# Gathering the two vectors of each retrieved expert by separate transfers into separate rings

## The chip, the cores and the metric

The kernel runs on one core of a Trainium2 chip. The metric is the device time of one execution in microseconds (us); less is better. The core's engines are TensorE (PE; its weight loads are listed as PEld), VectorE (DVE), ScalarE (ACT), GpSimd (POOL) and SyncE (SP), and 16 DMA engines move data between the chip's main memory and the on-chip memory.

## The reference, cut to what matters

One layer on 1024 tokens of width 1024: a token mixer (projection, convolution branch, stick-breaking attention, gates, output projection, layer norm) gives `x1`, and then a retrieval of single-neuron experts works on it. The change touches only the retrieval:

```
for each block of 128 tokens:                      # 8 blocks
    for each head:                                 # 8 heads
        idx, gate = top 16 of 128*128 product keys # per token
        u  = expert_u[idx]                         # 16 rows of 1024 float32 per token
        vv = expert_v[idx]                         # 16 rows of 1024 float32 per token
        act = gelu(dot(x1, u))
        y += sum over the 16 of gate * act * vv
    x = layer_norm(alpha * x1 + y)
```

Each token has its own experts, so nothing is reused between tokens.

## The kernel before

**Stages.** The first 890 us compute `x1`: projections, convolution, attention, gates. From there to the end runs the retrieval: 8 token blocks x 8 heads = 64 heads (`t` counts them), each with 16 slots (`s`), so 1024 slots in all. The 128 tokens of a block lie on the 128 partitions.

**One slot.** `expert_u` and `expert_v` are concatenated on the host to rows of 2048 floats (`uv_d`). GpSimd issues one indirect transfer for each slot (L477): 128 rows of 8 KB, one for each partition, 1 MB, into slot `s % 8` of `ring`, 8 x 8 KB a partition (`RING` = 8). VectorE multiplies the u half by `x1` and sums it (L1190, `dots`, which writes the product over the u half), two slots for each signal `dots_done`. ScalarE applies gelu and the gate (L911, L913) and writes a diagonal matrix of the weights (L920). TensorE multiplies this diagonal with the v half (L672, `experts`, two matmuls of 512 columns for each slot) and adds to `y` in PSUM, then signals `expert_used[s % 8]`. GpSimd waits for that signal before it fills the ring's slot again, so that a slot is held until both its dot product and its matmuls are done. Each gather goes through `wait_alone`, a wait on a register's value.

**Indices.** GpSimd turns the 16 indices of a head into integers in two casts of 8 (L472) and waits for each. The indices of head `t + 1` are found during head `t`: TensorE makes queries and scores between its expert matmuls (`queries` L648, `query_transposes` L656, `scores` L664), and VectorE finds the top 16 between its dot products: `topk_half` after slots 5 and 7, `topk_pairs` after slot 9, `expert_index` after slot 11, whose last instruction (L1177) releases GpSimd.

**Block ends.** After the 16 slots of a block's last head VectorE waits for TensorE's last matmuls and does the second layer norm (`finish`, L1201, L1114 to L1121). In block 0 the heads also carry the output projection (`wout_mm`, L631) and first layer norm (`x1_block`) of the next blocks, and SP loads 1 MB of query weights and 0.5 MB of `x` for each head.

Of the kernel before, what the change touches and what calls it, by code (L numbers as in the profile page):

```python
# [30 lines left out]
D = 1024  # L31
# [3 lines left out]
HALF = 512  # L35
# [9 lines left out]
TOPK = 16  # L45
# [3 lines left out]
RING = 8  # L49
DIAGS = 4  # L50
START = 1
KB = 256


C_A, C_G, C_Q, C_K = 0, CC, 2 * CC, 3 * CC
# [47 lines left out]
    return (0, 1, 2, 3, 6, 7)[u % Z_BANKS]  # L103


def build(nc, xT_d, x_d, w_proj_d, w_v_d, w_mix_d, w_out_d, w_q_d, keys_d, uv_d, cols_d, bv_d,
          b_out_d, ln1_g_d, ln1_b_d, ln2_g_d, ln2_b_d, out_d):
    ctx = ExitStack()
    with ctx:
# [22 lines left out]
        def at(kib, *shape):  # L132
            n = math.prod(shape)
            arena, first = (arena_low, 0) if kib < LOW else (arena_high, LOW)
            flat = arena[:, int((kib - first) * KB):int((kib - first) * KB) + n]
            if len(shape) == 1:
                return flat
            if len(shape) == 2:
                return flat.rearrange("p (a b) -> p a b", b=shape[1])
            return flat.rearrange("p (a b c) -> p a b c", b=shape[1], c=shape[2])  # L140
# [63 lines left out]
        q_nat = at(63, 2 * P)  # L204
        gates = at(57, NB, PH * TOPK)
        w_q = at(64, PH, KD, 2 * P)
        ring = at(128, RING, 2 * D)
        idx_f = at(192, TOPK)
        top_v = at(192.25, 2, TOPK)
        soft = at(193, TOPK)  # L210
# [110 lines left out]
        shifted = sem("shifted")  # L321
        exp_ready = sem("exp_ready")
        gates_ready = sem("gates_ready")
        gathered = [sem(f"gathered{r}") for r in range(RING)]
        dots_done = sem("dots_done")
        gelu_step = sem("gelu_step")
        diag_ready = sem("diag_ready")
# [78 lines left out]
        @block.gpsimd  # L406
        def _(pool):
            for s in (psum_read + expert_used + mixed +
                      [pre_read, wout_done, conv_done, att_done, sp_done, suffix_done, av_done, acc_done, out_read, z_done, x1_ready, q_ready,
                       qT_ready, score_ready, y_read, idx_ready, idx_copied, x1T_psum]):  # L410
                pool.sem_inc(s, START)
            pool.sem_inc(stored, 16 * START)
            pool.memset(conv_in[:, 0:PAD], 0.0).then_inc(pad_ready, 1)
            pool.memset(mean_w, 1.0 / CONV).then_inc(consts, 1)
            pool.memset(one_row[0:1, :], 1.0).then_inc(consts, 1)
            pool.memset(neg_ones, -1.0).then_inc(consts, 1)
            pool.memset(zeros[:, :], 0.0).then_inc(consts, 1)
            pool.memset(tri, -1.0).then_inc(pool_step, 1)
            pool.iota(iota_i[:, :], pattern=[[1, TOPK]], base=0, channel_multiplier=0).then_inc(consts, 1)
            pool.wait_ge(pool_step, 1)  # L420
            pool.affine_select(out=tri, in_=tri, compare_op=ALU.is_ge, fill=0.0, base=0,
                               pattern=[[-1, P]], channel_multiplier=1).then_inc(consts, 1)


            for j in range(4):
                pool.wait_ge(w1_rounded, j + 1)
                nc.gpsimd.tensor_tensor(w1_lo_r[:, j, :, :], w_ring[:, j, :, :], w1_hi_r[:, j, :, :].bitcast(F32),
                                        ALU.subtract).then_inc(w1_split, 1)
            with pool.Fori(1, CC) as it:
                for j in range(4):  # L430
                    wait_alone(pool, w1_rounded, it * 4 + j + 1, consts)
                    nc.gpsimd.tensor_tensor(w1_lo_r[:, j, :, :], w_ring[:, j, :, :], w1_hi_r[:, j, :, :].bitcast(F32),
                                            ALU.subtract).then_inc(w1_split, 1)
            for k in range(KD):
                pool.wait_ge(wv_rounded, k + 1)
                nc.gpsimd.tensor_tensor(wv_lo_r[:, k, :], w_v[:, k, :], wv_hi_r[:, k, :].bitcast(F32),
                                        ALU.subtract).then_inc(wv_split, 1)

            pool.wait_ge(var_done, 1)
            pool.wait_ge(psum_read[3], START + 6)
            pool.memset(q_pair[DH:P, 0, :], 0.0).then_inc(q_zeroed, 1)
            pool.memset(q_pair[0:DH, 1, :], 0.0).then_inc(q_zeroed, 1)
            with pool.Fori(0, PAIRS) as p:
                order = sorted([(u, 0) for u in DIAG_NO] + [(u + 1.5, 1) for u in DIAG_NO])
                for key, what in order:
                    u = int(key) if what == 0 else int(key - 1.5)
                    Q, kb, hd = UNITS[u]
                    c0 = kb * P - Q * HALF  # L450
                    if what == 0:
                        wait_alone(pool, sp_done, START + p * NU + u + 1, consts)
                        tile, signal = sp[:, u % 3, c0:c0 + P], sp_masked
                    else:
                        wait_alone(pool, att_done, START + p * NU + u + 1, consts)
                        tile, signal = att[:, u % 3, c0:c0 + P], att_masked
                    pool.affine_select(out=tile, in_=tile, compare_op=ALU.is_gt, fill=0.0, base=0,  # L457
                                       pattern=[[1, P]], channel_multiplier=-1).then_inc(signal, 1)


            pool.memset(ident, 0.0).then_inc(pool_step, 1)
            pool.wait_ge(pool_step, 2)
            pool.affine_select(out=ident, in_=ident, compare_op=ALU.not_equal, fill=1.0, base=0,
                               pattern=[[-1, P]], channel_multiplier=1).then_inc(consts, 1)


            with pool.Fori(0, NB * PH) as t:
                wait_alone(pool, idx_ready, START + t + 1, consts)
                for s in range(TOPK):
                    if s % RING == 0:  # L470

                        pool.tensor_copy(idx_now[:, s:s + RING],  # L472
                                         idx_f[:, s:s + RING]).then_inc(idx_copied, 1)
                        wait_alone(pool, idx_copied, START + t * 2 + (s // RING + 1), consts)

                    wait_alone(pool, expert_used[s % RING], START + t * 2 + s // RING, consts)
                    pool.indirect_dma_start(  # L477
                        out=ring[:, s % RING, :], out_offset=None, in_=uv_d,
                        in_offset=bass.IndirectOffsetOnAxis(ap=idx_now[:, s:s + 1], axis=0),
                    ).then_inc(gathered[s % RING], 16)  # L480


        @block.tensor
        def _(pe):
# [182 lines left out]

            def experts(t, g):
                for s in range(2 * g, 2 * g + 2):
                    pe.wait_ge(diag_ready, t * TOPK + s + 1)  # L670
                    for h in range(2):
                        last = nc.tensor.matmul(ps[:, 4 + h, :], diag[:, s % DIAGS, :],  # L672
                                                ring[:, s % RING, D + h * HALF:D + (h + 1) * HALF],
                                                start=False, stop=False, skip_group_check=True)
                    last.then_inc(expert_used[s % RING], 1)

# [57 lines left out]
        def _(act):  # L734
# [171 lines left out]

            def expert_weights(t, g, steps):

                act.wait_ge(dots_done, t * (TOPK // 2) + g + 1)
                s0 = 2 * g  # L910
                steps.link(nc.scalar.activation(gcol[:, s0:s0 + 2], hcol[:, s0:s0 + 2], ACT.Gelu))  # L911
                for s in (s0, s0 + 1):
                    last = nc.scalar.activation(wcol[:, s:s + 1], gcol[:, s:s + 1], ACT.Copy,  # L913
                                                scale=gates_flat[:, bass.ds(t * TOPK + s, 1)])
                steps.link(last)
                for s in (s0, s0 + 1):

                    f = s - DIAGS
                    act.wait_ge(expert_used[f % RING], START + t * 2 + (f // RING + 1 if f >= 0 else 0))
                    nc.scalar.activation(diag[:, s % DIAGS, :], ident, ACT.Copy,  # L920
                                         scale=wcol[:, s:s + 1]).then_inc(diag_ready, 1)
# [62 lines left out]
        def _(dve):  # L984
# [201 lines left out]

            def dots(b, t, g):
                for s in range(2 * g, 2 * g + 2):
                    dve.wait_ge(gathered[s % RING], (t * 2 + (s // RING + 1)) * 16)
                    last = nc.vector.scalar_tensor_tensor(  # L1190
                        out=ring[:, s % RING, 0:D], in0=x1[:, b, :], scalar=1.0, in1=ring[:, s % RING, 0:D],
                        op0=ALU.mult, op1=ALU.mult, accum_out=hcol[:, s:s + 1])
                last.then_inc(dots_done, 1)

# [112 lines left out]
```

## Time and profile before

| | |
|---|---|
| median of 3 runs | 3706.95 us (3705.57 to 3712.73) |
| profiled execution, span first to last instruction | 3699.8 us |
| median less span: what lies around it | 7.15 us |
| busy in the span | PE 84%, DVE 61%, ACT 37%, POOL 36% |
| DMA | 1133.49 MB, mean 306 GB/s over the span |

The profile gives the profiled execution by its span alone. Its page lists busy time, groups of instructions by source line with the idle time before them and what ended it, and the DMA queues. Busy time doesn't count the issuing and waiting of an engine, and a DMA_INDIRECT of POOL is the time in which GpSimd prepares a gather, not the transfer itself. The trace also answers with waits, timelines and busy time by window.

### The profile page before, as it was taken

How to read it: one execution, taken by the hardware profiler on the slowest of the kernel's cores; microseconds unless marked ns; L12 is line 12 of the kernel's file. 1: busy time of each engine (PE TensorE's matmuls, PEld its weight loads, DVE VectorE, ACT ScalarE, POOL GpSimd, SP SyncE). 2: the span in 40 equal slices, each digit the busy share in tenths (PEclk: the TensorE clock that was granted, in tenths of full speed). 3: DMA queues.
4: the chain of work that ended last, by engine and by line, in shares of the span. 5: the costliest groups of instructions: out<-in, count | busy, mean ns of one | idle time of the engine just before them, and what ended most of it. 6: DMA issues, size and time to landing. Idle time of an engine off the chain costs nothing. (4 is left out here: it accounts for less than half of the span.)

```text
span 3699.8 us, 39202 instructions
## 1 busy us (share of the span) xinstructions
PE 3119.5 (84%) x8608; PEld 1576.3 (43%) x8608; DVE 2257.1 (61%) x4803; ACT 1372.5 (37%) x3639; POOL 1341.2 (36%) x1320
## 2 busy tenths in 40 slices
PE   9989999996999888878887888788788878877886
PEld 7754436663444333333333333334333334333332
DVE  6973331113777666666666676666667666666765
ACT  3117761111444333333433333343333433333342
POOL 2301110001444344434444444444344534444443
PEclk9999999997999999999999999999999999999999
DMA  3000001106999999999999999999999989998998
GB/s 143 28 17 1 0 13 38 51 17 251 376 382 383 392 374 410 401 375 392 400 408 362 400 412 396 368 401 408 381 389 408 403 362 405 409 407 354 406 395 338
DMA packets 158001, 1133.49 MB, mean 306 GB/s; under 512 B 17554, under 2 KB 17682, under 8 KB 23443
## 3 DMA queue, kind: packets, MB, share of 16 engines
q0 software_dynamic: 147456, 1073.81, 71.4%
q1 hardware_dynamic: 10514, 59.34, 4.2%
q8 instruction: 12, 0.20, 0.0%
q14 instruction: 19, 0.15, 0.0%
HBM read 1128.88 MB, written 4.19 MB: 306 GB/s over the span
## 5 line engine op out<-in xcount | busy, mean ns | idle before, releaser
L672 PE MATMUL ps<-arena_high 128*128 128x512 f32 x4096 | 1942.0, 620 | 486.0 <-ACT arena_high L920 485.7
L477 POOL DMA_INDIRECT arena_high<-uv_dram,idx_now x1024 | 1138.6, 1112 | 1165.6 <-PE ps L672 926.8
L1190 DVE SCALAR_TENSOR_TENSOR arena_high<-arena_low,arena_high 128x1024 f32<-128x1024 f32 x1024 | 1225.1, 1223 | 546.3 <-DMA arena_high<-uv_dram,idx_now 525.9
L672 PEld LDWEIGHTS ps<-arena_high 128*128 128x128 f32 x4096 | 769.6, 196 | 1544.5 <-issue 795.2
L911 ACT ACTIVATE gcol<-hcol 128x2 f32<-128x2 f32 x512 | 103.6, 202 | 1167.3 <-DVE arena_high L1190 1166.6
L472 POOL CAST idx_now<-arena_high 128x8 uint32<-128x8 f32 x128 | 96.3, 753 | 748.0 <-DVE arena_high L1177 747.8
L920 ACT ACTIVATE arena_high<-arena_high,wcol 128x128 f32<-128x128 f32 x1024 | 355.2, 394 | 32.8
L913 ACT ACTIVATE wcol<-gcol,arena_low 128x1 f32<-128x1 f32 x1024 | 245.5, 286 | 71.2 <-ACT gcol L911 9.4
L648 PE MATMUL ps<-arena_low 128*128 (+1 forms) x1024 | 240.0, 389 | 12.7 <-ACT arena_low L886 10.0
L648 PEld LDWEIGHTS ps<-arena_low 128*128 128x128 f32 x1024 | 198.5, 195 | 65.3 <-issue 37.1
L174 PE MATMUL ps<-x_hi_bytes,w_bytes 128*128 128x512 f32 x512 | 200.3, 391 | 0.0
L1007 DVE SCALAR_TENSOR_TENSOR arena_low<-arena_low,cols 128x1024 f32 x120 | 177.8, 1482 | 17.5 <-DVE arena_low L1003 0.6
L911 ACT ACT_TABLE_LOAD x120 | 154.0, 1283 | 4.3 <-issue 1.7
L1145 DVE MAX8 arena_high<-arena_low 128x8 f32<-128x128 f32 x128 | 37.5, 293 | 180.5 <-ACT arena_low L899 180.5
L1036 DVE SCALAR_TENSOR_TENSOR arena_low<-ps,arena_low 128x512 f32<-128x512 f32 (+3 forms) x96 | 53.6, 558 | 144.8 <-ACT arena_low L814 144.8
L1089 DVE SCALAR_TENSOR_TENSOR arena_low<-ps,cols,arena_low 128x512 f32<-128x512 f32 x16 | 12.0, 751 | 197.7 <-PE ps L619 197.7
L631 PE MATMUL ps<-arena_low 128*128 128x512 f32 x256 | 116.5, 600 | 7.7 <-DMA arena_low<-w_out_dram 7.7
L899 ACT ACTIVATE arena_low<-ps 128x256 f32<-128x256 f32 x64 | 24.5, 383 | 249.7 <-PE ps L664 249.7
L457 POOL TENSOR_SCALAR_AFFINE_SELECT arena_low<-arena_low 128x128 f32<-128x128 f32 x128 | 40.9, 330 | 199.9 <-ACT arena_low L822 101.7
L619 PE MATMUL ps<-arena_low,arena_high 128*128 128x512 f32 x256 | 112.4, 592 | 0.0
L172 PE MATMUL ps<-x_hi_bytes,w_hi_bytes 128*128 128x512 f32 x256 | 101.2, 395 | 12.1 <-DVE x_lo_bytes L989 8.8
L172 PE MATMUL ps<-x_hi_bytes,w_bytes 128*128 128x512 f32 x256 | 105.8, 413 | 3.0 <-DVE w_bytes L1081 3.0
(144 smaller groups left out, 2776.1 us busy)
## 6 DMA issues: line engine op xcount, KB each, us to landing
arena_high<-uv_dram,idx_now POOLq DMA_INDIRECT x1024, 11.0
arena_low<-w_q_dram SPq DMA_DIRECT2D x15, 1024.0 KB, 11.2
arena_high<-w_mix_dram SPq DMA_DIRECT2D x8, 1536.0 KB, 6.4
arena_high<-w_proj_dram SPq DMA_DIRECT2D x16, 512.0 KB, 3.3
arena_high<-xT_dram SPq DMA_DIRECT2D x8, 512.0 KB, 7.8
arena_low<-w_out_dram SPq DMA_DIRECT2D x2, 2048.0 KB, 9.5
arena_low<-x_dram SPq DMA_DIRECT2D x8, 512.0 KB, 7.7
out_dram<-arena_low SPq DMA_DIRECT2D x8, 512.0 KB, 7.8
```

The costliest lines, as they stand in the source:

```text
L172: nc.tensor.matmul(out, w_hi, x_hi, start=first, stop=False)
L174: return nc.tensor.matmul(out, w_lo, x_hi, start=False, stop=last)
L477: pool.indirect_dma_start(out=ring[:, s % RING, :], out_offset=None, in_=uv_d, in_offset=bass.IndirectOffsetOnAxis(ap=idx_now[:, s:s + 1], ...
L619: last = nc.tensor.matmul(ps[:, 4 * h + 2 + y, :], w_mix[:, 1 - j, o:o + P], src[:, k, cs], start=(k == 0), stop=(k == CC - 1))
L631: last = nc.tensor.matmul(ps[:, 6 + h, :], mix_blk[:, k, :], w_out[:, k, h * HALF:(h + 1) * HALF], start=(k == 0), stop=(k == KD - 1))
L648: last = nc.tensor.matmul(ps[:, 2, 0:2 * P], x1T[:, k, :], w_q[:, place, k, :], start=(k == 0), stop=(k == KD - 1))
L672: last = nc.tensor.matmul(ps[:, 4 + h, :], diag[:, s % DIAGS, :], ring[:, s % RING, D + h * HALF:D + (h + 1) * HALF], start=False, stop=Fa ...
L911: steps.link(nc.scalar.activation(gcol[:, s0:s0 + 2], hcol[:, s0:s0 + 2], ACT.Gelu))
L913: last = nc.scalar.activation(wcol[:, s:s + 1], gcol[:, s:s + 1], ACT.Copy, scale=gates_flat[:, bass.ds(t * TOPK + s, 1)])
L920: nc.scalar.activation(diag[:, s % DIAGS, :], ident, ACT.Copy, scale=wcol[:, s:s + 1]).then_inc(diag_ready, 1)
L1007: ins = nc.vector.scalar_tensor_tensor(out=conv[:, c, :], in0=conv_in[:, k:k + S], scalar=cols[:, bass.ds(c * TAPS + (C_CW + k), 1)], in1= ...
L1190: last = nc.vector.scalar_tensor_tensor(out=ring[:, s % RING, 0:D], in0=x1[:, b, :], scalar=1.0, in1=ring[:, s % RING, 0:D], op0=ALU.mult, ...
```

## The change

The concatenated table becomes two, `u_d` and `v_d`, and the ring two rings of eight slots of 4 KB a partition, in the same memory. Each slot is gathered by two indirect transfers of 128 rows of 4 KB: u, then v, each with its own wait in front. The u transfer waits for the dot products of eight slots earlier (`dots_done`, which starts at 4 so that the first eight pass), the v transfer for `expert_used` as before. TensorE gets a wait on the v transfer, VectorE waits on the u transfer, and ScalarE's wait is shifted by the start value.

```
+DOTS_START = RING // 2
-        ring = at(128, RING, 2 * D)
+        u_ring = at(128, RING, D)
+        v_ring = at(160, RING, D)
-        gathered = [sem(f"gathered{r}") for r in range(RING)]
+        u_in = [sem(f"u_in{r}") for r in range(RING)]
+        v_in = [sem(f"v_in{r}") for r in range(RING)]
+            pool.sem_inc(dots_done, DOTS_START)
...
+                    wait_alone(pool, dots_done, DOTS_START + t * (TOPK // 2) + ((s - RING) // 2 + 1), consts)
+                    pool.indirect_dma_start(
+                        out=u_ring[:, s % RING, :], out_offset=None, in_=u_d,
+                        in_offset=bass.IndirectOffsetOnAxis(ap=idx_now[:, s:s + 1], axis=0),
+                    ).then_inc(u_in[s % RING], 16)
                     wait_alone(pool, expert_used[s % RING], START + t * 2 + s // RING, consts)
                     pool.indirect_dma_start(
-                        out=ring[:, s % RING, :], out_offset=None, in_=uv_d,
+                        out=v_ring[:, s % RING, :], out_offset=None, in_=v_d,
                         in_offset=bass.IndirectOffsetOnAxis(ap=idx_now[:, s:s + 1], axis=0),
-                    ).then_inc(gathered[s % RING], 16)
+                    ).then_inc(v_in[s % RING], 16)
...
+                    pe.wait_ge(v_in[s % RING], (t * 2 + (s // RING + 1)) * 16)
                     pe.wait_ge(diag_ready, t * TOPK + s + 1)
                     for h in range(2):
                         last = nc.tensor.matmul(ps[:, 4 + h, :], diag[:, s % DIAGS, :],
-                                                ring[:, s % RING, D + h * HALF:D + (h + 1) * HALF],
+                                                v_ring[:, s % RING, h * HALF:(h + 1) * HALF],
...
-                act.wait_ge(dots_done, t * (TOPK // 2) + g + 1)
+                act.wait_ge(dots_done, t * (TOPK // 2) + (DOTS_START + g + 1))
...
-                    dve.wait_ge(gathered[s % RING], (t * 2 + (s // RING + 1)) * 16)
+                    dve.wait_ge(u_in[s % RING], (t * 2 + (s // RING + 1)) * 16)
                     last = nc.vector.scalar_tensor_tensor(
-                        out=ring[:, s % RING, 0:D], in0=x1[:, b, :], scalar=1.0, in1=ring[:, s % RING, 0:D],
+                        out=u_ring[:, s % RING, :], in0=x1[:, b, :], scalar=1.0, in1=u_ring[:, s % RING, :],
                         op0=ALU.mult, op1=ALU.mult, accum_out=hcol[:, s:s + 1])
```

## Rows read from the trace of the kernel before

**Rows 1.** The page: groups by line, then packets of POOL's own DMA queue.

```profile
L672 PE MATMUL ps<-arena_high 128*128 128x512 f32 x4096 | 1942.0, 620 | 486.0 <-ACT arena_high L920 485.7
L477 POOL DMA_INDIRECT arena_high<-uv_dram,idx_now x1024 | 1138.6, 1112 | 1165.6 <-PE ps L672 926.8
L1190 DVE SCALAR_TENSOR_TENSOR arena_high<-arena_low,arena_high 128x1024 f32<-128x1024 f32 x1024 | 1225.1, 1223 | 546.3 <-DMA arena_high<-uv_dram,idx_now 525.9
...
L472 POOL CAST idx_now<-arena_high 128x8 uint32<-128x8 f32 x128 | 96.3, 753 | 748.0 <-DVE arena_high L1177 747.8
...
q0 software_dynamic: 147456, 1073.81, 71.4%
```

**Rows 2.** Windows: us, busy of each engine, PEclk, DMA share, GB/s.

```profile
1340.00:1675.00 335.00, 271.52 (x686) 126.05 (x685) 223.60 (x525) 124.92 (x373) 145.23 (x140) 0.96 0.97 396
...
2032.00:2056.00 24.00, 18.83 (x46) 7.77 (x44) 17.37 (x50) 6.67 (x25) 9.89 (x8) 1.00 1.01 423
2058.48:2099.70 41.22, 34.05 (x87) 15.71 (x86) 27.16 (x65) 16.09 (x48) 19.61 (x18) 0.98 0.98 398
2016.00:2021.00 5.00, 5.00 (x9) 2.00 (x8) 5.00 (x8) 1.82 (x6) 3.13 (x3) 0.67 0.35 107
```

**Rows 3.** Timeline of POOL, first casts of heads 0, 1, 9, 17, 57 and 63.

```profile
892.24 0.19 POOL L472 CAST idx_now<-arena_high 128x8 uint32<-128x8 f32 x1 [369.17 <-DVE arena_high L1177]
937.66 1.05 POOL L472 CAST idx_now<-arena_high 128x8 uint32<-128x8 f32 x1 [3.27 <-DVE arena_high L1177]
...
1330.61 1.04 POOL L472 CAST idx_now<-arena_high 128x8 uint32<-128x8 f32 x1 [6.67 <-DVE arena_high L1177]
...
1674.64 1.04 POOL L472 CAST idx_now<-arena_high 128x8 uint32<-128x8 f32 x1 [6.57 <-DVE arena_high L1177]
...
3387.78 1.05 POOL L472 CAST idx_now<-arena_high 128x8 uint32<-128x8 f32 x1 [6.57 <-DVE arena_high L1177]
...
3637.15 1.04 POOL L472 CAST idx_now<-arena_high 128x8 uint32<-128x8 f32 x1 [6.58 <-DVE arena_high L1177]
```

**Rows 4.** Source line L477 over the whole trace.

```profile
L477 POOL DMA_INDIRECT arena_high<-uv_dram,idx_now x1024: 932/938/1977, 893.5 to 3670.6; - x171
...
DMA to landing us min/median/max: 5.4/11.0/27.3
```

**Rows 5.** Timeline: gathers that follow each other, first without, then with a dot product beside.

```profile
1721.62 0.94 POOL L477 DMA_INDIRECT arena_high<-uv_dram,idx_now  x1 [0.30 <-PE ps L672]
...
1722.87 0.94 POOL L477 DMA_INDIRECT arena_high<-uv_dram,idx_now  x1 [0.31 <-issue]
...
1724.11 0.94 POOL L477 DMA_INDIRECT arena_high<-uv_dram,idx_now  x1 [0.30 <-issue]
...
2024.54 1.23 DVE L1190 SCALAR_TENSOR_TENSOR arena_high<-arena_low,arena_high 128x1024 f32<-128x1024 f32 x1 [1.78 <-DMA arena_high<-uv_dram,idx_now]
2024.68 1.90 POOL L477 DMA_INDIRECT arena_high<-uv_dram,idx_now  x1 [0.31 <-issue]
...
2026.88 0.93 POOL L477 DMA_INDIRECT arena_high<-uv_dram,idx_now  x1 [0.30 <-PE ps L672]
```

**Rows 6.** Timeline: first cast of head 26 and its neighbours; eight gathers that follow it.

```profile
2013.63 0.17 DVE L1166 TENSOR_SCALAR top_i<-top_i 128x16 uint32<-128x16 uint32 x1
...
2015.82 0.69 DVE L1177 TENSOR_REDUCE arena_high<-arena_low 128x16 f32<-128x512 f32 x1 [0.27 <-DVE arena_low L1173]
...
2018.61 1.00 POOL L477 DMA_INDIRECT arena_high<-uv_dram,idx_now  x1 [0.92 <-POOL idx_now L472]
...
2029.36 1.12 POOL L477 DMA_INDIRECT arena_high<-uv_dram,idx_now  x1 [0.30 <-issue]
2030.48 0.20 POOL L472 CAST idx_now<-arena_high 128x8 uint32<-128x8 f32 x1
```

**Rows 7.** Windows, columns as in Rows 2: one head of block 0, and loads of 4 KB rows at the start.

```profile
1033.20:1080.96 47.76, 45.58 (x119) 21.81 (x119) 34.74 (x76) 20.01 (x52) 21.17 (x19) 1.00 0.95 384
...
2.00:8.00 6.00, 0.00 (x0) 0.00 (x0) 1.41 (x1) 2.57 (x4) 3.88 (x9) 1.00 1.00 361
```

More of the change, by code:

```diff
@@ L103, in z_bank, with build @@
     return (0, 1, 2, 3, 6, 7)[u % Z_BANKS]
-def build(nc, xT_d, x_d, w_proj_d, w_v_d, w_mix_d, w_out_d, w_q_d, keys_d, uv_d, cols_d, bv_d,
+def build(nc, xT_d, x_d, w_proj_d, w_v_d, w_mix_d, w_out_d, w_q_d, keys_d, u_d, v_d, cols_d, bv_d,
           b_out_d, ln1_g_d, ln1_b_d, ln2_g_d, ln2_b_d, out_d):
@@ L1290 @@
         "keys": np.stack([arr(peer_keys_1), arr(peer_keys_2)], axis=1).transpose(3, 0, 1, 2).reshape(P, PH * 2 * NKEY),
-        "uv": np.concatenate([arr(peer_u), arr(peer_v)], axis=1),
+        "u": arr(peer_u),
+        "v": arr(peer_v),
         "cols": np.concatenate([col(bi[0:col_v]), col(bi[col_g:]), col(arr(conv_b_pw2)), col(arr(conv_b_dw)),
```

## The prediction

> **What bounds the kernel now.** I read the page's groups first, then the source line of the gathers, then windows of the retrieval stage, then timelines of single heads. The page names TensorE as busiest, but its matmuls wait 486 us for ScalarE's diagonals, those for the dot products, and the dot products wait 525.9 us for gathers [rows 1]. GpSimd waits 926.8 us for TensorE to free a slot and is busy 1138.6 us with 1024 gathers [rows 1]. The reader is to see a closed loop, and has to ask what fills it. The windows answer: over 335 us the 16 DMA engines are busy 0.97 of the time at 396 GB/s, and away from the head's start 1.01 at 423 GB/s [rows 2]. The DMA engines are the bound of an ordinary head. The only hole is at the head's start, where GpSimd has issued all gathers it has indices for and sits idle 6.57 us until L1177 [rows 3]; over 5 us there the DMA share falls to 0.35 in the worse head, 0.98 over another whole head [rows 2].
>
> The first casts of the heads give the clock of the stage: heads 9 to 17 take 1674.64 - 1330.61 = 344.0 us for eight, and heads 9 to 57, six blocks, 3387.78 - 1330.61 = 2057.2 us, or 42.86 us a head, block ends included. Within a block it is (3637.15 - 3387.78)/6 = 41.56 us. Block 0 and the turn to block 1 take 1330.61 - 892.24 = 438.4 us for nine heads, 48.7 each [rows 3].
>
> **What earlier freeing can give.** The bytes stay: 1073.81 MB / 64 = 16.78 MB a head [rows 1]. At the 423 GB/s of the full stretch [rows 2] that is 39.7 us a head. The most that a better ring can give is thus 41.56 - 39.7 = 1.9 us in an ordinary head and 3.2 us a head with block ends spread over it. Freeing u early by itself gives none of this where the queues of the DMA engines are full already; it gives some where GpSimd can run ahead over a block's end.
>
> **What the change adds on GpSimd.** Each head now needs 32 gathers instead of 16, in one in-order stream. A gather's own time is 0.938 us in the median [rows 4]. Where nothing holds it back, gathers start 1.245 us apart (1721.62, 1722.87, 1724.11), because 0.30 us of issue lie between them [rows 5]. The new gather brings its own wait on a register's value, exactly like the old one, so both parts count twice. 32 x 1.245 = 39.8 us a head. Before, 16 x 1.245 = 19.9 us were hidden under the DMA engines' 40 us; now they are not.
>
> Does a gather of half the bytes cost half? It has the same 128 rows and index count; queue 0 counts 147456 / 1024 = 144 packets a gather, of 1073.81 MB / 147456 = 7.3 KB in the mean [rows 1], so a row goes as one piece, and half rows leave the number the same. No row shows a 4 KB gather; the bounds are 0.938 (by rows gathered) and 0.469 us (by bytes), and I take the first because the row count is all that GpSimd handles and it never touches the data.
>
> Casts: two a head. The first costs 0.2 us at the best, and 0.92 us pass to the next gather instead of 0.30 [rows 3, 6]; so 0.2 + 0.62 = 0.8 us each, 1.6 us a head. In the mean the cast takes 0.753 us [rows 1], 0.55 more, 1.1 us a head.
>
> Port: a gather beside a dot product takes longer. The dot product runs 2024.54 to 2025.77, the gather starts 0.14 us after it and takes 1.90 us, ending 0.81 us after the dot product does; the next, with none beside its start, takes 0.93 [rows 5]. The mean gather is 1.112 us against the median 0.938, 0.174 more [rows 1, 4]. Dot products still are 16 x 1.22 us a head, so the chance that a gather meets one stays nearly the same while gathers double: 32 x 0.174 = 5.6 us. From below I bound this by zero (landings may fall into step with the issues, so that they miss each other), from above by the eight gathers from 2018.61 to 2029.36, 1.536 us apart [rows 6]: 32 x 0.291 = 9.3 us. I take 5.6, the mean over all 1024.
>
> The Trainium skill says as much, in "SBUF — State Buffer", "Who interferes with whom": a VectorE instruction with two inputs in SBUF blocks a GpSimd instruction that reads SBUF, for its whole length. The trace agrees (1.90 us beside a 1.23 us dot product). By that rule with every dot product blocking one gather by half its length the lock would cost 16 x 0.61 = 9.8 us a head, by the rows 5.6.
>
> Sum for GpSimd: 39.8 + 1.6 + 1.1 + 5.6 = **48.1 us a head**, without any wait for data. It exceeds the 39.7 us of the DMA engines and the 41.56 of now.
>
> **The other queues.** TensorE is busy 34.05 us and VectorE 27.16 us of an ordinary head of 41.22 us [rows 2]; both stay below 48. The new wait of TensorE on v stands in front of the matmuls, and behind it queue the next head's queries and scores. The v gather is issued some 1.4 us after the u gather, while dot product (1.22), gelu, weight and diagonal take longer than that, so v is there when the diagonal is: nothing. The index chain: u of slot 11 is issued as gather 23 of 32, so nine gathers with their gaps, 9 x 1.41 = 12.7 us, are still GpSimd's own before it wants new indices. In that time must go the landing, the dot product of 1.2 us, and 2013.63 to 2016.51 = 2.9 us of indexing [rows 6]. The shortest landing now is 5.4 us for 1 MB [rows 4]; with a DMA load of 16.78 MB / 48.1 us = 349 GB/s there is little queueing. 5.4 + 1.2 + 2.9 = 9.5 us is hidden by 3 us. So I expect GpSimd's 6.57 us of idle at the head's start gone, and nothing in its place; if landings exceed 8.6 us that cover is gone and each us more costs one a head.
>
> Block ends: the six blocks cost 6 x (8 x (42.86 - 41.56)) = 62 us over their ordinary heads, for the layer norm on VectorE. GpSimd with 16 transfers of room, 16 x 1.41 = 22.6 us, runs through that; I put it at zero after. Block 0: TensorE busy 45.58 us of a head of 47.76 [rows 7]; GpSimd's 48.1 is close to it. 9 x 48.1 = 433 against 438.4 now; with both so close I take no change.
>
> **The sum.** Six blocks: 48 x (48.1 - 42.86) = +252 us. The last seven heads: 7 x (48.1 - 41.56) = +46. Block 0 and everything before 892 us: 0. Together +298 us. Against the profiled span, 3699.8 + 298 = 3998; the 7.15 us around it stay: **4005 us** against 3706.95, 8.0% slower.
>
> **Rivals.**
> A, the forecast: GpSimd's issue becomes the bound, 48.1 us a head. Chance 0.80. With the port at its upper bound, 51.8 us a head: 48 x 8.9 + 7 x 10.2 + 9 x 3.1 = +527, 4234 us. With half the port's cost, 45.3 us: 117 + 26 = +143, 3850 us.
> B, the same bound with gathers and dot products falling into step, 42.5 us a head at most (39.8 + 1.6 + 1.1): 48 x (-0.4) + 7 x 0.9 = -11 us; with the casts undisturbed too, 41.4: -71, about 3636 us. It speaks for it that runs of gathers at 1.245 us exist; against it, 1.112 in the mean. Chance 0.06.
> C, the one on the other side: a gather of half the bytes costs GpSimd less. It decides at a mean spacing of (42.86 - 2.7)/32 = 1.255 us, port included, where A has 1.419; with 0.469 + 0.30 + 0.174 = 0.94 us GpSimd needs 33 us and the DMA engines are the bound again, without holes: 48 x (39.7 - 42.86) + 7 x (39.7 - 41.56) = -165 us, 3542 us. Against it: same rows, same packets. Chance 0.07.
> D, the DMA engines themselves slow down with 4 KB rows: at the start of the kernel loads of such rows ran at 361 GB/s with a share of 1.00 [rows 7], the lowest full rate I found, start-up included. 16.78 / 361 = 46.5 us a head: 48 x 3.6 + 7 x 4.9 = +207, 3914 us, if GpSimd were faster than that. Chance 0.07.
> The Trainium skill asks for at least 1 MiB a transfer ("DMA: Bandwidth & Descriptors", "Bandwidth"); that is D's rule, and these transfers fall to half of it. No row before shows gathers below 1 MB.
>
> **How the numbers follow.** Less than 0.2% (7 us) can't be told from no change here. Slower: A, D and a little of B: 0.87. Faster: C and most of B: 0.11. Same: 0.02. The range of A, 3850 to 4234, holds D too; taking in some in-step behaviour on the low side I give 3800 to 4210.
>
> **What would show it.** Right: GpSimd busy about 2048 x 1.11 = 2280 us, over 80% of the retrieval; nearly all idle in front of its gathers "issue", none for TensorE or L1177; DMA share near 0.85 to 0.9 and some 350 GB/s; dot products waiting longer for gathers; landings below 8 us. Wrong: a median below 0.9 us for a 4 KB gather (C), DMA share of 1.0 at under 380 GB/s with GpSimd waiting for slots (D), GpSimd still idle some us a head for L1177 (the index chain, and heads beyond 50 us), or spacings of 1.25 us throughout (B).

## The result, and the profile after

The changed kernel takes 4051.13 us (median of 4 runs, 4048.09 to 4054.41) against 3706.26 us for the kernel before on the same chip: ratio **1.0924**, 95% interval 1.0908 to 1.0939. It was run again later beside an experiment, with ratio 1.0914 (1.0900 to 1.0928). The forecast was 4005 us, 8% slower; the measured time is 46 us above it and inside the range.

The page of the changed kernel, its groups by line and POOL's own queue, answering to [rows 1]:

```profile
L682 PE MATMUL ps<-arena_high 128*128 128x512 f32 x4096 | 2031.2, 644 | 734.4 <-ACT arena_high L930 733.5
L1200 DVE SCALAR_TENSOR_TENSOR arena_high<-arena_low,arena_high 128x1024 f32<-128x1024 f32 x1024 | 1242.4, 1224 | 958.3 <-DMA arena_high<-u_dram,idx_now 940.6
...
L481 POOL DMA_INDIRECT arena_high<-u_dram,idx_now x1024 | 1172.4, 1145 | 391.9 <-issue 265.8
L486 POOL DMA_INDIRECT arena_high<-v_dram,idx_now x1024 | 1191.7, 1164 | 325.2 <-issue 302.8
...
L476 POOL CAST idx_now<-arena_high 128x8 uint32<-128x8 f32 x128 | 42.8, 334 | 377.7 <-DVE arena_high L1187 377.4
...
q0 software_dynamic: 294912, 1073.87, 72.6%
```

GpSimd now prepares 2048 gathers of 1145 and 1164 ns, 2364 us in all, where it had 1024 of 1112 ns, 1139 us. The dot products' wait for gathers has grown from 525.9 to 940.6 us, and TensorE's wait for diagonals from 485.7 to 733.5: everything behind GpSimd is starved. The bytes are the same, and a gather now lands 6.1 us after its issue in the median, where it took 11.0 [rows 4].

Who GpSimd waits for in the changed kernel, whole trace:

```profile
POOL idx_now L476 <- DVE arena_high L1187: 377.4, 6, 371.2
POOL arena_high L486 <- issue: 302.8, 977, 2.0
POOL arena_high L481 <- issue: 265.8, 870, 1.1
POOL arena_high L481 <- POOL idx_now L476: 116.0, 126, 0.9
...
POOL arena_high L486 <- PE ps L682: 18.5, 34, 7.7
POOL arena_high L481 <- PE ps L682: 7.0, 23, 0.3
...
POOL arena_high L481 <- DVE arena_high L1200: 1.9, 1, 1.9
```

The reader is to see that GpSimd hardly waits for anybody any more. Of the 377.4 us for indices 371.2 is the one wait before the first head; for TensorE it waits 25.5 us, where it was 926.8 [rows 1]; for the dot products, the new release, 1.9 us in all. What is left is "issue", the gap of some 0.3 us that every gather has in front of it.

A stretch of POOL's timeline, with the second cast of a head in the middle of it:

```profile
2011.35 1.78 POOL L486 DMA_INDIRECT arena_high<-v_dram,idx_now  x1 [0.30 <-issue]
2013.44 1.36 POOL L481 DMA_INDIRECT arena_high<-u_dram,idx_now  x1 [0.30 <-issue]
2015.10 0.94 POOL L486 DMA_INDIRECT arena_high<-v_dram,idx_now  x1 [0.30 <-issue]
2016.34 0.94 POOL L481 DMA_INDIRECT arena_high<-u_dram,idx_now  x1 [0.30 <-issue]
2017.58 1.87 POOL L486 DMA_INDIRECT arena_high<-v_dram,idx_now  x1 [0.30 <-issue]
...
2027.71 0.20 POOL L476 CAST idx_now<-arena_high 128x8 uint32<-128x8 f32 x1
2028.84 0.96 POOL L481 DMA_INDIRECT arena_high<-u_dram,idx_now  x1 [0.93 <-POOL idx_now L476]
```

A 4 KB-row gather takes 0.94 us undisturbed, exactly what an 8 KB-row gather took [rows 5], and others are stretched, as before, in these lines to 1.36 to 1.87 us; the runs with `x1` in PSUM below show that the dot products do it.

First casts of heads 0, 9 and 57, answering to [rows 3]:

```profile
896.15 0.19 POOL L476 CAST idx_now<-arena_high 128x8 uint32<-128x8 f32 x1 [371.25 <-DVE arena_high L1187]
1356.50 1.05 POOL L476 CAST idx_now<-arena_high 128x8 uint32<-128x8 f32 x1 [0.29 <-DVE arena_high L1187]
3690.26 1.05 POOL L476 CAST idx_now<-arena_high 128x8 uint32<-128x8 f32 x1 [0.28 <-DVE arena_high L1187]
```

They split the 346.5 us between the two spans (4046.3 against 3699.8):

| stretch | before, us | after, us | difference | forecast |
|---|---|---|---|---|
| start to first cast | 892.2 | 896.2 | +3.9 | 0 |
| heads 0 to 9 | 438.4 | 460.4 | +22.0 | 0 |
| heads 9 to 57 | 2057.2 (42.86 a head) | 2333.8 (48.62) | +276.6 | +252 (48.1) |
| head 57 to the end | 312.0 | 356.0 | +44.0 | +46 |

The work before the first cast is the same in both, and the +3.9 us there is scatter: in the late release below the first cast starts at 892.95 us, in the kernel with small second gathers at 896.14.

One reading of the windows did not come out as forecast. Changed kernel, columns as in [rows 2]:

```profile
1340.00:1675.00 335.00, 255.52 (x626) 117.42 (x624) 203.51 (x480) 115.27 (x342) 257.51 (x240) 0.95 0.96 353
```

The DMA share is 0.96, the same as before within 0.01, while GB/s fell from 396 to 353. By the share alone the DMA engines would look full. The experiments had to tell whether they were.

### The profile page after: what moved, and what is told of

Read it like the earlier page. It is cut to its first block and busy times, and to the rows that moved or that the text cites. A ratio compares the mean times of both kernels' runs of the same rounds, so it can differ in the third digit from the quotient of the medians.

```text
span 4046.3 us, 41919 instructions
## 1 busy us (share of the span) xinstructions
PE 3217.9 (80%) x8608; PEld 1608.5 (40%) x8608; DVE 2274.2 (56%) x4803; ACT 1370.6 (34%) x3639; POOL 2513.4 (62%) x2344
## 5 line engine op out<-in xcount | busy, mean ns | idle before, releaser
L682 PE MATMUL ps<-arena_high 128*128 128x512 f32 x4096 | 2031.2, 644 | 734.4 <-ACT arena_high L930 733.5
L1200 DVE SCALAR_TENSOR_TENSOR arena_high<-arena_low,arena_high 128x1024 f32<-128x1024 f32 x1024 | 1242.4, 1224 | 958.3 <-DMA arena_high<-u_dram,idx_now 940.6
L682 PEld LDWEIGHTS ps<-arena_high 128*128 128x128 f32 x4096 | 799.1, 204 | 1857.4 <-ACT arena_high L930 981.0
L481 POOL DMA_INDIRECT arena_high<-u_dram,idx_now x1024 | 1172.4, 1145 | 391.9 <-issue 265.8
L486 POOL DMA_INDIRECT arena_high<-v_dram,idx_now x1024 | 1191.7, 1164 | 325.2 <-issue 302.8
L476 POOL CAST idx_now<-arena_high 128x8 uint32<-128x8 f32 x128 | 42.8, 334 | 377.7 <-DVE arena_high L1187 377.4
```

The costliest lines, as they stand in the source:

```text
L481: pool.indirect_dma_start(out=u_ring[:, s % RING, :], out_offset=None, in_=u_d, in_offset=bass.IndirectOffsetOnAxis(ap=idx_now[:, s:s + 1] ...
L486: pool.indirect_dma_start(out=v_ring[:, s % RING, :], out_offset=None, in_=v_d, in_offset=bass.IndirectOffsetOnAxis(ap=idx_now[:, s:s + 1] ...
L1200: last = nc.vector.scalar_tensor_tensor(out=u_ring[:, s % RING, :], in0=x1[:, b, :], scalar=1.0, in1=u_ring[:, s % RING, :], op0=ALU.mult, ...
```

## The experiments

Heads 9 to 57 are given as us a head, from the first casts as above. Each ratio is to the kernel before, in runs on the same chip.

**A second gather of 64 B rows, in the kernel before.** This adds GpSimd's work without the bytes and without the split.

```
                     ).then_inc(gathered[s % RING], 16)
+                    wait_alone(pool, expert_used[s % RING], START + t * 2 + s // RING, consts)
+                    pool.indirect_dma_start(
+                        out=extra[:, s % RING, :], out_offset=None, in_=ex_d,
+                        in_offset=bass.IndirectOffsetOnAxis(ap=idx_now[:, s:s + 1], axis=0),
+                    ).then_inc(extra_in[s % RING], 16)
```

> The kernel before (one 8 KB-row gather a slot), with a second gather a slot of rows of 64 B into a spare corner, waited for by the dot products; all of the computation stays. If GpSimd's issue of 2048 gathers is what bounds the changed kernel, this must come out like it: 47 to 50 us a head, 3950 to 4080 us, GpSimd busy near 2350 us. If the 4 KB rows are what costs (slower DMA engines), only some small packets are added here and the time stays within 3705 to 3780 us.

Measured: 4052.34 us, ratio 1.0908 (1.0885 to 1.0931), 48.71 us a head: the changed kernel's loss, whole. Its groups:

```profile
L479 POOL DMA_INDIRECT arena_high<-uv_dram,idx_now x1024 | 1164.8, 1137 | 391.2 <-issue 302.3
L484 POOL DMA_INDIRECT arena_high<-ex_dram,idx_now x1024 | 1205.8, 1178 | 317.0 <-issue 296.3
```

A gather of 8 KB in all (128 rows of 64 B) costs GpSimd as much as one of 1 MB. The cost goes by the gather, or by its rows, and not by its bytes.

**Half the bytes.** The changed kernel with 2 KB rows (the v gather and the v table are cut in the same way):

```
-                        out=u_ring[:, s % RING, :], out_offset=None, in_=u_d,
+                        out=u_ring[:, s % RING, 0:HALF], out_offset=None, in_=u_d,
...
-        "u": arr(peer_u),
+        "u": arr(peer_u)[:, 0:512],
```

> The changed kernel with rows of 2 KB instead of 4 KB: only the first half of each expert vector is gathered, the other half of both rings is zeroed once (some 20 to 60 us, once), so half of the dot product and of the output is left out; all instructions stay. If GpSimd's issue is the bound, halving the bytes changes nothing beyond the zeroing: 4050 to 4120 us, gather median still 0.94 us. If the DMA engines are the bound (share 0.96 in the changed kernel), their work halves and it falls to 3600 to 3850 us.

Measured: 4086.25 us, ratio 1.0992 (1.0960 to 1.1024), 49.39 us a head. One window of it, columns as in [rows 2]:

```profile
1340.00:1675.00 335.00, 251.31 (x607) 115.25 (x606) 195.39 (x454) 112.27 (x332) 258.83 (x230) 0.94 0.58 169
```

With the DMA engines at 169 GB/s and a share of 0.58 the kernel is no faster, even 0.6% slower. The DMA engines are therefore not its bound, and neither are they the changed kernel's, in spite of the share of 0.96. The zeroing is little of the 0.6%: the first cast starts 6.5 us later. In heads 9 to 57 the kernel takes 36.9 us more than the changed one, and its 1536 gathers there take 39.9 us more: the v gathers 1.283 us in the mean against 1.164, the u gathers 1.076 against 1.143. So the time follows GpSimd even here.

**4 KB rows with GpSimd relieved.** The v vectors are loaded by SyncE, from fixed rows:

```
-                    pool.indirect_dma_start(
-                        out=v_ring[:, s % RING, :], out_offset=None, in_=v_d,
-                        in_offset=bass.IndirectOffsetOnAxis(ap=idx_now[:, s:s + 1], axis=0),
-                    ).then_inc(v_in[s % RING], 16)
...
+            def v_slots(t, s0, s1):
+                for s in range(s0, s1):
+                    sp_eng.wait_ge(expert_used[s % RING], START + t * 2 + s // RING)
+                    sp_eng.dma_start(v_ring[:, s % RING, :], v_d[s * P:(s + 1) * P, :]).then_inc(v_in[s % RING], 16)
```

> The changed kernel with the v transfers taken off GpSimd: SyncE loads 128 fixed rows of 4 KB of the v table into each v slot, so the retrieved v vectors are left out of the computation; the u gathers stay and wait for the expert matmuls. Same bytes, all in rows of 4 KB, 16 gathers a head on GpSimd. If GpSimd's issue is the bound, the time returns to the kernel before: 3600 to 3760 us. If rows of 4 KB make the DMA engines the bound by themselves (16.78 MB a head at 350 to 366 GB/s = 46 to 48 us), it stays at 3870 to 4010 us.

Measured: 3774.13 us, ratio 1.0159 (1.0144 to 1.0175), between the two forecasts. The casts say where the 1.6% lies: heads 0 to 9 take 512.3 us against 438.4, but heads 9 to 57 take 42.84 us a head, against 42.86 before. The loss is in block 0, where this variant puts SyncE's v loads in one queue with the query weights and `x` and their waits. The trace bears that out: TensorE's query matmuls wait 92.1 us there for the query weights, in 7 waits, where the kernel before has 2.6 us of such waits in all. That this is the whole 74 us isn't shown. A window that lies mostly in its block 2:

```profile
1675.00:2010.00 335.00, 266.58 (x678) 122.67 (x676) 225.17 (x530) 127.63 (x376) 152.55 (x142) 0.98 1.00 394
```

All bytes go in 4 KB rows, at 394 GB/s, and the pace is the old one. Rows of 4 KB cost nothing by themselves here (half of them, SyncE's, lie one behind the other in memory; the other half are gathered), and 16 gathers a head instead of 32 give the whole loss of heads 9 to 57 back.

**Late release.** The changed kernel with the u transfer waiting for the expert matmuls:

```
-                    wait_alone(pool, dots_done, DOTS_START + t * (TOPK // 2) + ((s - RING) // 2 + 1), consts)
+                    wait_alone(pool, expert_used[s % RING], START + t * 2 + s // RING, consts)
```

> The changed kernel with the early release undone: the u transfer waits for the expert matmuls of eight slots earlier, as the v transfer does. If GpSimd never waits for a slot (it waited 18 to 20 us in all for TensorE in the changed kernel), the early release is worth nothing: within 0.2% of 4051 us. If the early release gives something back that the doubled issue hides, this is slower, by 0.3 to 2% (4063 to 4130 us).

Measured: 4027.28 us, ratio 1.0850 (1.0827 to 1.0874): faster than the changed kernel, if by less than 1%, and on another chip. So both were run beside each other.

> The changed kernel itself again, beside the next run on the same chip: 4040 to 4060 us, ratio 1.090 to 1.095 to the kernel before.

> The late release again (u waits for the expert matmuls), on the same chip as the changed kernel. If the 0.7% between 1.0924 and 1.085 is the chip's, both ratios now agree within 0.3%. If the early release itself costs time although GpSimd is the bound, the late one is again 0.4 to 0.8% faster.

Measured: changed kernel 4044.34 us, 1.0914 (1.0900 to 1.0928); late release 4036.38 us, 1.0885 (1.0867 to 1.0903). The difference is 0.3%, and the intervals touch. The early release gains nothing; whether it costs 0.3% is open.

**One wait for both gathers.** The late release, with the v gather following the u gather without a wait of its own:

```
                     ).then_inc(u_in[s % RING], 16)
-                    wait_alone(pool, expert_used[s % RING], START + t * 2 + s // RING, consts)
                     pool.indirect_dma_start(
                         out=v_ring[:, s % RING, :], out_offset=None, in_=v_d,
```

> The changed kernel with late release and a single wait for each slot's two gathers: the v gather follows the u gather with no wait between. If the 0.30 us between gathers is the cost of the wait on a register's value, 1024 of them fall to 0.1 us or less and the time falls by up to 200 us, to 3850 to 3900 us. If the gap belongs to the gather itself, it stays 0.30 us and the time stays within 1% of 4027 us.

Measured: 4097.25 us, ratio 1.1048 (1.1031 to 1.1066). The group of its v gathers:

```profile
L485 POOL DMA_INDIRECT arena_high<-v_dram,idx_now x1024 | 1174.2, 1147 | 318.0 <-issue 304.3
```

304.3 us over 1024 gathers are 0.30 us each, with no wait in front. The gap belongs to the gather, not to the wait. That it came out 1.5% slower than the late release with both waits (1.0885) was not expected. ScalarE's waits before L899, which copies the queries, show something that no kernel so far had:

```profile
  remote: 81.0, 18
  PE ps L656: 46.4, 23
```

"Remote" means that the trace names no releaser for the signal that ended the wait. There are 55 such waits of ScalarE in this run, 214.3 us in all, and 28 of GpSimd, 36.8 us; the kernel before, the changed kernel and the late release have none. Heads 9 to 57 take 49.75 us a head against 48.54 with both waits, 58 us more: 29 of them are GpSimd's "remote" waits, 15 its longer waits for indices. What these waits are shows better in the next runs.

**x1 in PSUM.** The dot products' second input is copied to two free PSUM banks once a block, from block 1 on, in the kernel before and in the changed one, and in the changed one with late release:

```
+            def to_psum(b):
+                nc.vector.tensor_copy(ps_flat[:, 6 * HALF:8 * HALF], x1[:, b, :]).then_inc(x1_moved, 1)
+                wait_alone(dve, x1_moved, b, consts)
...
-                        out=ring[:, s % RING, 0:D], in0=x1[:, b, :], scalar=1.0, in1=ring[:, s % RING, 0:D],
+                        out=ring[:, s % RING, 0:D], in0=x1_in, scalar=1.0, in1=ring[:, s % RING, 0:D],
```

> The kernel before with x1 copied to two free PSUM banks once per block, from block 1 on, so that the dot products have one input in on-chip SBUF memory and one in PSUM; all of the computation stays. If the dot products' two SBUF inputs are what delays GpSimd, the first cast of a head falls from 1.05 to 0.2 us and no gather takes over 1 us from 1280 us on; the hole in the DMA engines at each head's start shrinks by up to 0.9 us: 3650 to 3700 us. If the delay has another cause, cast and gathers stay as they are and the time stays within 0.3% of before. If the PSUM read is slower than the SBUF read, the dot product takes over 1.3 us and the kernel is no faster.

Measured: 3713.62 us, ratio 1.0023 (1.0014 to 1.0032). Its gathers from 1400 to 3600 us:

```profile
L478 POOL DMA_INDIRECT arena_high<-uv_dram,idx_now x819 | 768.5, 938 | 1073.8 <-PE ps L673 927.4 <-issue 99.3 <-POOL idx_now L473 47.1
```

The mean is now 938 ns, the old median [rows 4], and the longest is 970 ns: the delay is gone, with the dot product at 1.22 us as before. So the delay is shown to come from the dot product's two SBUF inputs. The Trainium skill has it in "SBUF — State Buffer", "Who interferes with whom" (two SBUF inputs on VectorE against a GpSimd read); the trace agrees, 1.103 us a gather in the same stretch with both in SBUF and 0.938 with one. But the kernel before gains nothing by it and is 0.2% slower: where GpSimd isn't the bound, its time is free.

> The changed kernel with x1 in PSUM from block 1 on, as above. GpSimd then needs 32 x 1.245 + 1.6 = 41.4 us a head where it now needs 48.9: 55 heads x 7.5 us off 4051 gives 3640 us if nothing else binds. If the DMA engines move 4 KB rows at no more than 399 GB/s (42 us a head, as with v loaded by SyncE), 3680 to 3720 us. If the delay of the gathers has nothing to do with the dot products' inputs, it stays above 4000 us.

> The run above with the early release undone (the u transfer waits for the expert matmuls of eight slots earlier). With GpSimd near to the DMA engines' pace a slot's release can matter: if the early release is worth something once issue is cheaper, this is slower than the run above by 0.3 to 2%. If the ring of eight was never what held the gathers, the two agree within 0.3%.

Measured: 4266.77 us, ratio 1.1509 (1.1493 to 1.1524), and with late release 4223.11 us, 1.1390 (1.1375 to 1.1406). None of what was expected of both fits: the gathers did become short, and yet the kernel is 5% slower than the changed one. Timeline of the first of these, at one head's first slots:

```profile
2047.06 3.62 PE L658 MATMUL ps<-arena_low 128*128 x16
...
2055.15 0.94 POOL L487 DMA_INDIRECT arena_high<-v_dram,idx_now  x1 [0.30 <-issue]
2056.09 0.20 POOL L477 CAST idx_now<-arena_high 128x8 uint32<-128x8 f32 x1
2057.20 0.95 POOL L482 DMA_INDIRECT arena_high<-u_dram,idx_now  x1 [0.91 <-POOL idx_now L477]
2060.63 0.38 ACT L901 ACTIVATE arena_low<-ps 128x256 f32<-128x256 f32 x1 [13.70 <-remote]
2061.43 0.94 POOL L487 DMA_INDIRECT arena_high<-v_dram,idx_now  x1 [3.28 <-remote]
```

ScalarE's L901 copies the queries and waits for nothing but the last of the 16 query matmuls. They end at 2050.7 by the trace; L901 starts at 2060.63. GpSimd, too, waits for a signal of TensorE at that time and goes on 0.8 us after ScalarE. In between lies a row of gathers, 1.245 us apart but for the cast between the last two, the last of which ends at 2058.15, 2.5 us before L901. The head before shows the same: last gather to 2007.0, L901 at 2009.52. ScalarE sits idle 556.6 us in the 49 waits of L901 that end so, and L901 starts 8.2 to 11.6 us after the query matmuls' end in them. With late release there are 43, 484.9 us, and ScalarE goes on some 3.2 us after the last gather's end.

**A shorter lead.** To test whether the unbroken row holds the signal back, u may lead by only four slots, with `x1` in PSUM and early release:

```
-   wait_alone(pool, dots_done, DOTS_START + t * (TOPK // 2) + ((s - RING) // 2 + 1), consts)
+   wait_alone(pool, dots_done, DOTS_START + t * (TOPK // 2) + ((s - RING // 2) // 2 + 1), consts)
```

> x1 in PSUM and early release, but u may run ahead of the dot products by four slots instead of eight, so GpSimd has to pause within a head. In the run with x1 in PSUM ScalarE saw the end of the query matmuls 11 us late, once a head, each time 2.5 us after GpSimd's unbroken row of gathers stopped. If the unbroken row of gathers is what holds TensorE's signals back, the late signal is gone here and the time falls from 4267 to 3700 to 3950 us. If the delay has another cause, ScalarE's 11 us stay and a shorter lead can only add: 4267 us or more.

Measured: 3889.06 us, ratio 1.0497 (1.0476 to 1.0518), 45.49 us a head instead of 52.70. The waits of L901:

```profile
L901 ACT ACTIVATE arena_low<-ps x64: 360/384/385, 879.7 to 3794.7; 128x256 f32<-128x256 f32 x64
its engine sat idle before it (us, times) until:
  PE ps L658: 62.3, 46
```

Not one wait of L901 for "remote" is left. A tighter wait on GpSimd makes the kernel 9% faster than the run above and 4% faster than the changed kernel. That the late signals hang on how GpSimd issues is shown, since one wait of GpSimd is all that differs. That an unbroken row is what holds them back isn't. From 1400 us on, the longest rows at 1.245 us spacing are 16 gathers in the run with late signals in most heads and 12 in this one with none. But the late release has one of 15 without late signals, and the run with one wait for both gathers has none longer than 12 and late signals all the same; there ScalarE goes on in the middle of a row (L899 at 2058.18 us, during a gather that starts at 2057.96). By which path they are held back is open.

**The indices two slots earlier, one gather a slot.**

```
                         topk_half(steps, 0)
-                    if g == 3:
                         topk_half(steps, 1)
-                    if g == 4:
+                    if g == 3:
                         topk_pairs(steps, r)
-                    if g == 5:
+                    if g == 4:
                         expert_index(steps, r)
```

> The kernel before, with one 8 KB gather a slot, and the search for the next head's indices moved forward by two slots: both halves after slot 5, pairs after slot 7, index after slot 9. GpSimd's 6.57 us of idle at each head's start and the hole in the DMA engines behind it shrink. If that hole is all that the kernel before had to give (1.9 us a head), 3590 to 3680 us. If the ring of eight slots, held until the expert matmuls, is the real limit, GpSimd waits for TensorE instead and the time stays within 0.3% of before.

Measured: 3691.60 us, ratio 0.9958 (0.9945 to 0.9971), a gain of 0.4%, the fastest version of the study. Who GpSimd waits for, 1400 to 3600 us:

```profile
POOL arena_high L477 <- PE ps L672: 921.7, 473, 13.6
```

Its casts' waits for L1177 after the first head fall from 379 to 56 us over the trace, and TensorE's release of slots takes their place: before all gathers of the trace 1213.9 us instead of 926.8 [rows 1]. The hole was only partly the indices'; the rest moved to the ring, and the windows give 396 GB/s from 1400 to 1800 us where the kernel before has 394.

## Why the prediction was right, point by point

**The bound moves to GpSimd: right, shown.** The second gather with hardly any bytes reproduces the loss (1.0908), half the bytes don't lower it (1.0992), and taking the second gather off GpSimd gives the old pace back (42.84 us a head).

**A gather costs by its rows, not its bytes: right.** 0.94 us in the median for rows of 4 KB and 8 KB (0.948 us for 64 B rows). By rows or by the gather as such wasn't separated, since every gather had 128 rows. Rival C falls.

**The sum of 48.1 us a head: 0.5 short of 48.62, by two terms off in opposite directions.** The port term was sized as 0.174 us a gather; the means of 1.145 and 1.164 less 0.940 give 0.215, or 6.9 us a head instead of 5.6. The prediction took the stretch of a gather to stay the same; it grew. The casts were sized as 0.753 us; they take 0.334, 0.8 us a head less. That most of one error made up for the other is luck. Rival B was the opposite bet. Dot products and gathers didn't fall into step of themselves; it took moving `x1`, and the floor of 41.4 us wasn't reached even then: with the full lead late signals came in (52.70 us a head), which nothing in the trace before showed, and with the short lead (45.49) GpSimd waits 209.7 us in heads 9 to 57 for dot products, 4.4 us a head.

**Block 0 at no change: the step that failed in size.** It gave +22 us. The prediction put GpSimd's 9 x 48.1 = 433 us beside the 438.4 of before and took no change; heads 0 to 9 run at 51.2 us. By the trace GpSimd's 288 gathers there take 1.175 us in the mean where the forecast had 1.112, 18 us more, and GpSimd waits 11.4 us for TensorE, which the forecast had at none. The trace before had a hint of the first: 1.152 us a gather in heads 0 to 9 against 1.101 in heads 9 to 57, where the sum took one mean for all. VectorE's layer norms there are two-input operations as well, which I had left out of GpSimd's time; that they are what stretches the gathers wasn't tested. The forecast span is 48 us short in all: 22 in block 0, 25 in heads 9 to 57, 4 of scatter at the start, less 2 in the last heads.

**The index chain and block ends at zero: right.** The waits of GpSimd's casts for L1187 after the first are 6.2 us in the whole trace. Landings were to stay below 8 us: they do in the median (6.1 us), with a longest of 20.6.

**Early release is worth nothing: right for this kernel.** GpSimd waits 1.9 us for dot products in all, and the late release is as fast or 0.3% faster. What early release would be worth were the gathers cheap stays open: the run made for it was spoiled by late signals.

**DMA share near 0.85 to 0.9: wrong.** It was 0.96 at 353 GB/s. The rate was right, the share isn't proportional to it. GpSimd's gathers were to keep it busy for over 80% of the retrieval; 2364 us of the 3150 from the first cast on are 75%, and the forecast's own 2280 us would have been 73%: a slip in the sum. I had also put rival D's price, 46.5 us a head, on a start-up row; 4 KB rows run at 394 GB/s and 42.84 us a head, so D had nothing to it. The Trainium skill's advice of 1 MiB a transfer ("DMA: Bandwidth & Descriptors", "Rules for kernel authors") holds for this kernel's time, but through GpSimd's fixed cost, not through the DMA engines' rate: at 512 KB a load they keep the pace.

## What to carry to other kernels

Before splitting a gather, multiply GpSimd's start-to-start spacing (here 1.245 us, and 1.45 beside two-input VectorE work) by the new count and compare it with the loop's period: a gather's price doesn't fall with its bytes. A buffer freed earlier can help only where the issuing engine waits for that buffer, and once it is itself the bound its wait list shows little but "issue". A DMA share near 1 doesn't prove that DMA is the bound: halve the bytes and see.

## What the runs showed of the hardware that had not been expected

The DMA share isn't in proportion to the bytes moved: 0.97 at 396 GB/s before, 0.96 at 353 GB/s after, 1.00 at 394 GB/s with v by SyncE, 0.58 at 169 GB/s with half rows. What it goes by wasn't tested.

TensorE's signals reached ScalarE some 10 us late, once in most heads, with `x1` in PSUM, while GpSimd issued gathers 1.245 us apart, and arrived 2.5 us after the last of them (3.2 with late release). With a tighter wait on GpSimd they came at once, and the kernel took 378 us less of 4267. They were late in 18 heads, by up to 10.4 us, also with `x1` in SBUF, where the wait between the two gathers of a slot was left out. The changed kernel, whose gathers also follow each other with 0.30 us between them over whole heads, had none.
